# Delta-rule token rows in one turn per tile, the softmax scale folded into a norm weight, and the first stream's keys in the last attention turns

## What is computed

```
proj = rms_norm(x) @ w_in                # conv q/k/v, b, a, z, attention q, k, v
# group A: gated delta rule, 4 heads
c = silu(causal_conv(conv_in)); q, k, v = split(c)
q = l2_norm(q) * 128 ** -0.5; k = l2_norm(k)
o, S = gated_delta_rule(q, k, v, g, beta, s0)       # block by block, carries S
# group B: differential attention, 4 heads, two maps
q = rope_partial(rms_norm(dq, q_norm)); k = rope_partial(rms_norm(dk, k_norm))
s = einsum('bqhmd,bshmd->bhmqs', q, k) * 64 ** -0.5
p = softmax(s); p = p[:, :, 0] - lam * p[:, :, 1]; o = p @ v
```

## Time and profile before

| | us |
|---|---|
| median of 3 runs (lowest, highest) | 1449.78 (1449.38, 1450.89) |
| profiled execution | 1448.19 |
| its span, first to last instruction | 1446.4 |
| PE busy in the span | 1363.7 |
| DVE busy | 896.0 |
| ACT busy | 676.2 |
| POOL busy | 364.3 |

### The profile page before, as it was taken

How to read it: one execution, slowest core, us unless ns; L and a number is a source line. 1 busy time by engine, 2 the same in 40 slices (tenths; PEclk the granted TensorE clock), 3 DMA queues, 4 the chain that set the end, 5 groups by cost and what they waited for, 6 DMA issues and landing times.

```text
span 1446.4 us, 24371 instructions
## 1 busy us (share of the span) xinstructions
PE 1363.7 (94%) x8677; PEld 1237.6 (86%) x8677; DVE 896.0 (62%) x1482; ACT 676.2 (47%) x1278; POOL 364.3 (25%) x240
## 2 busy tenths in 40 slices
PE   5999999999998999999998878789999999999999
PEld 5999999988786998787777765568999999998787
DVE  5977767644446666646555766745787777754534
ACT  6555555533335453534345542543555555543332
POOL 2555555500000000121221421000555555510000
PEclk9999999999998999999999999999999999999999
DMA  6222222270100422110023016670132222244000
GB/s 197 83 83 82 80 85 87 87 296 9 29 0 19 142 75 75 59 59 29 30 74 118 1 50 199 233 262 0 59 88 87 87 87 87 87 139 181 35 2 36
DMA packets 139318, 127.27 MB, mean 88 GB/s; under 512 B 3845, under 2 KB 107909, under 8 KB 139260
## 3 DMA queue, kind: packets, MB, share of 16 engines
q1 hardware_dynamic: 136748, 117.15, 25.4%
q0 software_dynamic: 2512, 9.34, 1.9%
HBM read 115.83 MB, written 10.39 MB: 87 GB/s over the span
## 4 chain that ended last, share of the span: by engine, by line
PE 87%; DVE 8%; ACT 2%; issue 2%; DMA 0%; POOL 0%; SPq 0%; DVEq 0%; ACTq 0%
PE psum_all L943 23%; PE psum_all L944 23%; PE psum_all L945 23%; PE psum_all L953 6%; PE psum_all L1853 2%; PE psum_all L1841 2%; PE psum_all L513 1%; PE psum_all L2119 1%; PE psum_all L1845 1%; PE psum_all L1790 1%; PE psum_all L1963 1%; PE psum_all L2146 0%; DVE x_norm L463 0%; DMA x_tok<-x_prompt 0%; PE psum_all L2282 0%
## 5 line engine op out<-in xcount | busy, mean ns | idle before, releaser
L943 PE MATMUL psum_all<-hw_hi,gu_op 128*128 128x320 f32 x1200 | 372.0, 310 | 2.5 <-DVE gu_op L580 2.5
L944 PE MATMUL psum_all<-hw_lo,gu_op 128*128 128x320 f32 x1200 | 371.9, 310 | 0.0
L945 PE MATMUL psum_all<-hw_hi,gu_op 128*128 128x320 f32 x1200 | 370.9, 309 | 0.0
L943 PEld LDWEIGHTS psum_all<-hw_hi,gu_op 128*128 128x128 f32 x1200 | 226.7, 189 | 3.1 <-DVE gu_op L580 2.7
L944 PEld LDWEIGHTS psum_all<-hw_lo,gu_op 128*128 128x128 f32 x1200 | 228.1, 190 | 0.0
L945 PEld LDWEIGHTS psum_all<-hw_hi,gu_op 128*128 128x128 f32 x1200 | 226.2, 189 | 0.0
L828 POOL TENSOR_TENSOR w_sum<-raw_gu 128x512 f32<-128x512 f32 x80 | 141.0, 1762 | 225.7 <-DVE gu_op L595 221.1
L595 DVE TENSOR_TENSOR gu_op<-w_sum,gu_op 128x512 fp32r<-128x512 f32 x160 | 160.4, 1003 | 56.6 <-ACT gu_op L591 51.4
L943 PE MATMUL psum_all<-wd_hi,a_hi 128*128 128x512 f32 x440 | 171.4, 390 | 1.7 <-DVE x_tok L961 1.7
L616 DVE TENSOR_TENSOR a_lo<-aT,a_hi 128x640 fp32r<-128x640 f32 x88 | 72.6, 825 | 160.5 <-ACT a_hi L608 160.5
L944 PE MATMUL psum_all<-wd_lo,a_hi 128*128 128x512 f32 x440 | 171.2, 389 | 0.0
(11 more groups left out here) (364 smaller groups left out, 2470.0 us busy)
## 6 DMA issues: line engine op xcount, KB each, us to landing
raw_gu<-ffn_w_gu SPq DMA_DIRECT2D x80, 512.0 KB, 4.6
wd<-ffn_w_down SPq DMA_DIRECT2D x2, 4096.0 KB, 20.8
raw_b<-w_in SPq DMA_DIRECT2D x8, 1024.0 KB, 5.3
wd<-ffn_w_down SPq DMA_DIRECT2D x2, 3584.0 KB, 12.5
raw_cv<-w_in SPq DMA_DIRECT2D x13, 512.0 KB, 3.9
wd<-ffn_w_down SPq DMA_DIRECT2D x6, 1024.0 KB, 5.0
K_c<-cache_k SPq DMA_DIRECT2D x6, 1024.0 KB, 7.9
V_c<-cache_v SPq DMA_DIRECT2D x6, 1024.0 KB, 5.9
```

The lines of the kernel that those rows point to most:

```text
L943: nc.tensor.matmul(out, lhs_hi, rhs_hi, start=start, stop=False, skip_group_check=True)
L944: nc.tensor.matmul(out, lhs_hi, rhs_lo, start=False, stop=False, skip_group_check=True)
L945: return nc.tensor.matmul(out, lhs_lo, rhs_hi, start=False, stop=stop, skip_group_check=True)
```

## The change

There are three edits.

1. `tok_pe`, `tok_dve` and `tok_act` lose one of their two yields per tile, so that the token rows take 6 turns instead of 11. VectorE now sums tile t-1 behind the copies of tile t; the last tile's sums stand in front of the first gate instructions. Everything that follows in delta stands five turns earlier against attention.
2. `q_norm`'s weight is multiplied by -1/8 once (one instruction on 128x64). The scores come out as the negative of the scaled ones, so the row maximum becomes a row minimum that is used as it is, the exponential has scale -1, and lines 2162 and 2392 go. The mask's constant changes its sign.
3. The keys of the first stream are transposed and copied in turns 41 and 42 of prompt attention (counted from 0); prompt attention has 43 turns instead of 44 and cache attention 33 instead of 35. The last unit's output goes to PSUM bank 4 and its copy stands right behind the last turn.

```diff
 def qk_dve(dve):
     dve.wait_ge(N["params_loaded"], 16 * 9)
+    V.tensor_scalar(qk_gain[:, 0, :], qk_gain[:, 0, :], -(DK ** -0.5), None, ALU.mult)\
+        .then_inc(N["q_gain"], 1)
...
 def tok_pe(pe):
...
                     last.then_inc(N["tok_tr"], 1)
                 yield
-                yield
...
 def tok_dve(dve):
+            def sums(t):
+                for w in range(2):
+                    dve.wait_ge(N["tok_sq"], 2 * t + w + 1)
+                    V.tensor_reduce(gates[:, G_SSQ + w, t, :], (kbg, kd)[w][:], AX.X, ALU.add)\
+                        .then_inc(N["tok_sums"], 1)
             for t in range(TT):
                 for w in range(3):
                     dve.wait_ge(N["tok_tr"], 3 * t + w + 1)
                     V.tensor_copy(tok[:, t, 4 * w:4 * w + 4, :],
                                   psum[GB[w]].rearrange("p (h d) -> p h d", d=P))\
                         .then_inc(N["tok_copied"], 1)
-                yield
-                for w in range(2):
-                    ...
-                yield
+                if t:
+                    sums(t - 1)
+                yield
+            sums(TT - 1)
...
+        FIRST_KEYS = {START[-1] + TURNED: 0, START[-1] + VALUES: 1}
+        def att_turns(stages, first_keys):
-            for turn in range(START[-1] + OUT + 1):
+            for turn in range(START[-1] + OUT):
                 for stage, do in stages:
                     if turn - stage in AT_TURN:
                         do(AT_TURN[turn - stage])
+                if turn in FIRST_KEYS:
+                    first_keys(FIRST_KEYS[turn])
                 yield
...
 def maximum(u):
-                link(dve, "att_chain", MAX_LINK[u],
-                     V.tensor_reduce(soft[:, 0:2], psum_all[:, s:s + 2, 0:n], AX.X, ALU.max))
-                V.tensor_scalar(soft[:, 2:4], soft[:, 0:2], -(DK ** -0.5), None, ALU.mult)\
+                V.tensor_reduce(soft[:, 2:4], psum_all[:, s:s + 2, 0:n], AX.X, ALU.min)\
                     .then_inc(N["nmax"], 1)
...
 def probs(u):
-                                         bias=soft[:, 2 + m:3 + m], scale=DK ** -0.5,
+                                         bias=soft[:, 2 + m:3 + m], scale=-1.0,
```

More of the change, by code:

```diff
@@ L2066, in qkT_act @@
             act.wait_ge(N["qbd_zero"], 1)
-            nc.scalar.activation(late_neg[:], const("early_neg"), ACT.Copy)\
+            nc.scalar.activation(late_neg[:], const("early_neg"), ACT.Copy, scale=-1.0)\
                 .then_inc(N["qkT_copied"], 1)
@@ L2150, in att_pe @@
             pe.wait_ge(N["qkT_copied"], 13)
-            yield from att_turns(((TURN, transposes), (VALUES, values), (SCORES, scores)))
+            yield from att_turns(((TURN, transposes), (VALUES, values), (SCORES, scores)),
+                                 lambda pair: cache_keys(pe, 0, pair))
         def att_dve(dve):
@@ L2177, in combine @@
                                        ALU.mult, ALU.add).then_inc(N["pcomb"], 1)
-            yield from att_turns(((MAXIMUM, maximum), (COMBINE, combine)))
-        def links():
-            n, of_max, of_combine = 1, {}, {}
-            for turn in range(START[-1] + OUT + 1):
-                if turn - MAXIMUM in AT_TURN:
-                    of_max[AT_TURN[turn - MAXIMUM]] = n
-                    n += 1
-                if turn - COMBINE in AT_TURN:
-                    of_combine[AT_TURN[turn - COMBINE]] = n
-                    n += 2
-            return of_max, of_combine
-        MAX_LINK, COMBINE_LINK = links()
+            yield from att_turns(((MAXIMUM, maximum), (COMBINE, combine)),
+                                 lambda pair: cache_key_dve(dve, 0, pair))
         def att_act(act):
@@ L2221, in out @@
                                      scale=inv_sum[:, u % 4, 0:1]).then_inc(N["pv_copied"], 1)
-            yield from att_turns(((TURNED, turned), (OUT, out), (PROBS, probs)))
+            yield from att_turns(((TURNED, turned), (OUT, out), (PROBS, probs)),
+                                 lambda pair: cache_key_act(act, 0, pair))
+            out(len(UNITS) - 1)
         def cache_sync(sp):
@@ L2262, in cache_sync, with cache_keys @@
                 load_values(b)
-        def cache_pe(pe):
-            def keys(b, heads):
-                pe.wait_ge(s_K[b % 3], (16, 16, 32)[b % 3] * (b // 3 + 1))
-                for h in heads:
-                    n = 4 * b + h
-                    if n >= 2:
-                        pe.wait_ge(N["kt_copied"], n - 1)
-                    for k in range(4):
-                        last = nc.tensor.transpose(psum[2 + n % 2][:, hc(k)], K_c(b % 3, k)[:, hc(h)],
-                                                   ident)
-                    last.then_inc(N["kt_mm"], 1)
+        def cache_keys(pe, b, pair):
+            pe.wait_ge(s_K[b % 3], (16, 16, 32)[b % 3] * (b // 3 + 1))
+            if b == 0 and pair == 0:
+                pe.wait_ge(N["pv_copied"], len(UNITS) - 1)
+            for h in (2 * pair, 2 * pair + 1):
+                n = 4 * b + h
+                if n >= 2:
+                    pe.wait_ge(N["kt_copied"], n - 1)
+                for k in range(4):
+                    last = nc.tensor.transpose(psum[2 + n % 2][:, hc(k)], K_c(b % 3, k)[:, hc(h)],
+                                               ident)
+                last.then_inc(N["kt_mm"], 1)
+        def cache_pe(pe):
             def scores(b):
@@ L2326, in cache_pe @@
                 if b + 1 < STREAMS:
-                    keys(b + 1, (0, 1))
+                    cache_keys(pe, b + 1, 0)
                 yield
@@ L2331, in cache_pe @@
                 if b + 1 < STREAMS:
-                    keys(b + 1, (2, 3))
+                    cache_keys(pe, b + 1, 1)
                 yield
```

75 lines of the change are left out of this document (31 added, 44 removed).

## The result

The changed kernel takes 1466.15 us (median of four runs, 1465.98 to 1472.01) against 1450.03 us for the kernel before: a ratio of 1.0118, with a 95% interval of 1.0101 to 1.0134. It is 16 us slower, where 3.5 us faster had been forecast and 1453.0 was the end of the range. The profiled execution has 1465.98 us and a span of 1464.2.

What follows compares the result with a forecast made beforehand. TensorE's own work plus its waits was taken as the bound; 5.6 - 1.1 - 3.2 - 1.0 - 1.2 - 2.0 - 0.6 = -3.5 us against 1448.2 gave 1444.7 (1446.3 on the runs' scale), range 1440.0 to 1453.0.

Steps and rivals of the forecast that it cites:

- A: Token rows and gates: TensorE waits 7.3 us for the gates' product instead of 2.26; +5.6 us, bounds +3 and +7.
- B: Tiles 1 and 2 in the projection turns: tile 1's 1.19 us wait goes; -1.1 us, between -2.5 and +1.
- C: Starts of tiles 3 and 4: shorter chains from state update through Xm, 1.2 and 2.0 us; -3.2, bounds 0 and -6.5.
- tile 4 gives nothing: Start of tile 4: if VectorE is held for all three POOL instructions each time, the tile-start term is -1.2 us.
- its sign for being right, 2.5 us: Start of tile 4: Xm comes within 2.5 us of the state update if the forecast is right.
- The clock: Slow stretches behind the waits of tiles 3 and 4: shorter waits may keep the clock up; -1.0 us, between 0 and -3.4.
- E: Prompt and cache attention lose three turns, five level steps move under projection matmuls, only gaps go; -2.0 us.
- D: Attention softmax: removing the -1/8 multiplication saves 0.19 us per stream on six of eight; -1.2 us, bounds 0 and -1.5.
- F: Tile 4's waits fall in turns with two more attention products; -0.6 us, between +1 and -1.5.
- the gate product's wait decides: Rival at the gates: that wait dominates, Xm's gain is lost again, turns give nothing; +3.3 us, 1453.1, chance 0.20.

Runs made afterwards that it cites:

- empty5: The changed kernel with five empty turns behind the gates on every engine; 1466.13 us, ratio 1.0096.
- front5: The changed kernel with five empty turns ahead of the gates instead of behind them; 1459.71 us, ratio 1.0054.
- scale_only: The kernel before with q's norm weight scaled, a minimum for maximum and multiplication, and scale -1.0 in the exponentials; 1450.61 us, ratio 0.9991.
- keys_only: The kernel before with only the first stream's keys moved into the prompt attention's last turns, three attention turns fewer; 1459.68 us, ratio 1.0050.
- keep_tok_s1: The kernel before with the second and third edits, token rows left at two turns per tile, one empty delta turn ahead of the streams; 1448.84 us, ratio 0.9978.
- empty1_s1: The changed kernel with one empty turn behind the gates and one more of delta work ahead of the streams; 1459.45 us, ratio 1.0061.
- after_s1: The changed kernel with one empty turn of the delta work ahead of the streams; 1475.10 us, ratio 1.0157.
- early_table: The changed kernel with a Silu of a constant behind tile 2's copy of Tm, loading ScalarE's table earlier; 1464.56 us, ratio 1.0079.

## Why the prediction was wrong

**A, token rows and gates (+5.6): right, slightly small.** The mechanism came as written. The gates' product started at 598.65, which is 594.9 plus the 3.7 us by which this execution was already late, and waited 7.01 us (7.3 forecast). VectorE found the split's input late twice, by 1.28 us each:

```profile
584.92 0.69 DVE L1399 TENSOR_TENSOR b_lo<-raw_b,b_hi 128x512 fp32r<-128x512 f32 x1 [1.28 <-ACT b_hi L1348]
...
592.86 0.69 DVE L1399 TENSOR_TENSOR b_lo<-raw_b,b_hi 128x512 fp32r<-128x512 f32 x1 [1.28 <-ACT b_hi L1348]
```

Measured as a whole it is 7.0 us against before (`empty5`) and 6.2 us against the same kernel with cover (`front5`), the slow clock included. The term's upper bound was 7.

**B, tiles 1 and 2 (-1.1): the waits went, and a larger one came.** Tile 1's 1.19 us is gone, as forecast, and 1.57 and 1.69 us became 1.34 and 1.09. The bound of +1, "if the projection's last copies then show a wait that it covers now", named the right place at a third of its size: 3.16 us for z, and ten microseconds at a clock of 0.69 behind it. I had priced the copies and not the table load ahead of them, and no slow clock.

**C, starts of tiles 3 and 4 (-3.2): the sum of waits came right by luck, and Xm of tile 4 was wrong.** The listed waits are 3.2 us less; a new one of 1.18 us for a unit's output, in front of Xm of tile 4, makes it 2.1. And the chain that was to become shorter hardly did: from the state update's start to TensorE's product with Rm it took 16.88 us before and 17.06 after at tile 3, 19.11 and 18.17 at tile 4, 0.2 more and 0.9 less where 1.2 and 2.0 less were forecast. The waits shrank more than the chain because other products now stand among them. Xm did not get in before GpSimd. VectorE in the trace after:

```profile
851.11 1.12 DVE L1712 SCALAR_TENSOR_TENSOR S_p<-S_p,gates,psum_all 128x128 f32<-128x128 f32 x4 [1.91 <-PE psum_all L1900]
852.15 0.68 DVE L1765 TENSOR_REDUCE gates<-LT 128x4 f32<-128x512 f32 x1
852.75 4.23 DVE L1657 TENSOR_TENSOR XR<-tok,gates 128x512 f32<-128x512 f32 x1
```

and GpSimd:

```profile
852.53 0.83 POOL L2699 DMA_DIRECT2D gdn_prompt<-S_p  x1 [13.33 <-DVE S_p L1712]
853.39 1.05 POOL L1774 TENSOR_TENSOR kbg<-tok,gates 128x512 f32<-128x512 f32 x1
854.38 1.04 POOL L1775 TENSOR_TENSOR tok<-tok,gates 128x512 f32<-128x512 f32 x1
855.38 1.04 POOL L1776 TENSOR_TENSOR kd<-tok,gates 128x512 f32<-128x512 f32 x1
```

Xm started 0.64 us before GpSimd's first multiplication and still ended 0.5 us behind its third: 4.23 us for an instruction that takes 0.68. It overlapped the DMA issue at 852.53 from its start; whether that holds it too can't be told from one row. The rule of the Trainium skill that the prediction weighed ("SBUF — State Buffer", Practical consequences: the loser waits for one whole instruction) is not what this row shows, nor what the earlier trace rows showed: three in a row held it. The case that the prediction named for this, "tile 4 gives nothing", did not follow in full either: Xm ended 5.87 us behind the start of the state update, 6.54 before, and its sign for being right, 2.5 us, was missed.

**The clock (-1.0): wrong in sign, by 7 us.** The same 2556 products kept TensorE busy for 6.1 us more; this lies inside what A, B and E cost and is not added to it. The prompt attention has 0.92 between its cuts and the kernel before 0.94, the cache attention 0.96 and 1.00. The slow stretches at tile 4 went, those behind the gates and at tile 3 grew, and those behind z and one stream's keys came. The term priced only the two waits that were to shrink, and gave the longer waits of A and of the shift no slow clock, but for 1.7 us in A's upper bound.

**D, the multiplication by -1/8 (-1.2): not contradicted.** `scale_only` measures -0.9 parts in a thousand, -1.3 us, inside its own noise. The last streams' periods, scores to scores and the last one to the output projection, are 7.13, 7.57 and 7.20 us after and 7.43, 7.57 and 7.39 before: 0 to 0.3 us each. `scale_only` has the same gains of 0.2 us, and one period that is 1.06 us longer at a lower clock takes them back.

**E, three turns fewer and five level steps moved (-2.0): this is the step that failed.** It is two things. The keys in the prompt attention's last turns did give something: 3.1 us in that part (`keys_only`, 116.95 to 113.85), some of it products that moved to the cache part, and 3.8 us over the three parts, with the second edit, where the cache offset is good (`keep_tok_s1`). The rest was counted as if time left the thin turns and the full ones took it in for nothing, "TensorE's work stays, so only gaps go". Two errors are in that sentence. First, moving a program earlier against another one does not empty a stretch: what leaves it at the front is replaced at the back by the steps that follow. Against `empty5`, 42 products left the prompt attention for the projections and 32 came in from the cache part. The streams start 1.06 us behind the cache's first scores after, and 5.72 us before. Second, the gaps depend on which steps share a turn, and the old pairing was better than the other ones that were run. No gaps went: the prompt attention has 19.0 us of idle time in both kernels, with 34 products fewer. What was forecast for the part from q's transposes to the cache's first scores was a gain; it lost 2.0 us against `empty5`, and the projections lost 6.0 us against it, of which 1.6 are idle time and most of the rest is the moved products' own. I looked at the new pairing only where tiles start, and priced the shift against the cache turns at nothing. The cost of that was small here, 1.9 us, only because five turns and three turns partly cancel: the shift of -5 and that of +3 are both odd, and +3 alone costs 11 us in `keys_only`.

**F, tile 4's waits among other products (-0.6).** It can't be separated from E.

Summed over the parts of the profiled executions: A 7.0, the shift in the projections 6.0, the prompt attention -0.8 (the keys' gain, less what the shift costs), the cache 1.9. That is 14.1 us; with 3.7 us from the start-up it is the 17.8 us between the spans. No edit touches the start-up, and over the sixteen programs the first SwiGLU matmul started between 20.40 and 24.09 us. With one trace of each, it can't be told whether that belongs to the single execution or to the program: five kernels with the token edit start at 23.2 us or later, the six others with it at 21.4 to 21.8, and those without it at 20.4 to 21.6. So up to 3.7 us of the measured loss may lie there. The medians differ by 16.1.

Of the rivals, "the gate product's wait decides" had the sign and the largest term, and half of its condition, a wait over 7 us at line 1627, was just met; the other half was not, since the wait before tile 4 fell from 5.29 to 2.78 us. It lacked the shift. That the shift is the missing term is shown by `empty1_s1` against `keep_tok_s1`, which have the same two later edits and a good cache offset each: 1.0061 against 0.9978, 12 us, of which the gates' cover is 6.2. What makes one pairing of turns better than another in the prompt attention stays open; odd against even was tried there and fell.

## What to carry to other kernels

When two hand-written programs are interleaved by counting turns, an edit that removes turns from one of them re-pairs everything behind it; price each later stage by which steps now share a turn and stand ahead of which copies, or put empty turns back where the pairing starts to matter and try the edit apart from its shift. A turn that does nothing on the engine that seems idle may be what covers a chain: the five "empty" turns here covered the gates for 6 us. Cut the span at fixed instructions before believing a sum: the median of `empty5` equalled that of the changed kernel to 0.02 us (ratios 1.0096 and 1.0118) while its parts moved by -6, -2 and +9 us. And look at the clock of the products behind a new wait: of the 14.1 us here, 6.1 were the same products at a lower mean clock.

## What the runs showed of the hardware

- A VectorE multiplication of 128x512 took 4.23 us across a GpSimd DMA issue and three GpSimd multiplications in a row, six times its 0.68 us.
- A table load of 1.28 us on ScalarE costs nothing or its whole length by what stands ahead of it in the list: moving it gave 1.42 us back.
- Behind a wait of 3.16 us for z the clock was 0.69 over 10 us with TensorE busy for 9.40 of them. Behind the same wait in `after_s1`, with the same instructions up to there, it was 0.83 over 10 us; behind 1.74 us in `early_table` also 0.83; and behind 2.78 us at tile 4 it stayed at 1.00. So the length of the wait alone did not decide it.
- The same 2556 products kept TensorE busy for 333.56 us at a mean clock of 0.98 and for 339.66 us at 0.96.
- Single executions of programs that are the same there differed by 3.7 us in the first 24 us, by 3.2 us from there to the token rows and by 4.1 us from the output projection on, each about as much as or more than this change was forecast to bring.
